# Four of the 24 modulation blocks weighed on VectorE instead of TensorE, in a two-block transformer kernel on one core

## What is computed

```python
ada = jax.nn.silu(c) @ w_ada[l] + b_ada[l]          # c: (1, 2048), w_ada: (2048, 12288)
sh1, sc1, gt1, sh2, sc2, gt2 = jnp.split(ada, 6, axis=-1)
h = modulate(rmsnorm(x, norm1_g[l]), sh1, sc1)
proj = h @ w_in[l]                                  # pool, k, v, indexer and q columns
...                                                 # indexer top-k, attention, multi-scale pool
mix = jnp.concatenate([attn_out, pool_out], axis=-1) @ w_out[l]
x = x + gt1[:, None, :] * mix
h2 = modulate(rmsnorm(x, norm2_g[l]), sh2, sc2)
x = x + gt2[:, None, :] * hier_moe(h2, w_grp[l], w_exp[l], w1[l], w3[l], w2[l])
```

## Time and profile before

| what | value |
|---|---|
| median of 3 runs | 2362.9 us (2359.02, 2363.03, 2362.9) |
| the profiled execution, its own time | 2358.78 us |
| its span | 2356.5 us |
| TensorE busy over the span | 2081.6 us (88%) |
| VectorE busy over the span | 1254.1 us (53%) |
| share of the ending chain | TensorE 49%, DMA 34%, VectorE 9% |
| TensorE modulation units in stage A | 672 matmuls into psO, 96 into psM |

### The profile page before, as it was taken

The page is one execution under the profiler, slowest core; times in us unless marked ns, Lnnn a source line. Parts: engine busy times, 40 slices in busy tenths (PEclk is TensorE's granted clock), DMA queues, the critical chain, the costliest instruction groups (busy, mean ns, idle before and its releaser), DMA issues.

```text
span 2356.5 us, 38378 instructions
## 1 busy us (share of the span) xinstructions
PE 2081.6 (88%) x14534; PEld 1353.8 (57%) x14534; DVE 1254.1 (53%) x2281; ACT 857.6 (36%) x1308; POOL 32.4 (1%) x32
## 2 busy tenths in 40 slices
PE   6899999989988888888888888999998999997997
PEld 2677767762222222222222223998887999997887
DVE  3546567554444444444444445558856554477655
ACT  3343344431111111111111114457854444466543
POOL 0000000000000000000000001011100000000000
PEclk9999999999999999999999999999998999999999
DMA  9998987889999999999999998553444455543442
GB/s 360 381 345 297 310 274 247 305 324 394 427 428 428 427 427 428 427 427 427 428 427 427 428 428 341 195 184 125 140 151 155 142 180 183 176 141 103 140 135 92
DMA packets 135046, 695.42 MB, mean 295 GB/s; under 512 B 14992, under 2 KB 15120, under 8 KB 85264
## 3 DMA queue, kind: packets, MB, share of 16 engines
q1 hardware_dynamic: 134928, 693.79, 76.5%
HBM read 691.63 MB, written 2.10 MB: 294 GB/s over the span
## 4 chain that ended last, share of the span: by engine, by line
PE 49%; DMA 34%; DVE 9%; ACT 4%; SPq 3%; issue 2%; DVEq 0%; ACTq 0%
PE acc L1174 33%; DMA ring<-in_w 30%; DMA land<-in_stream_a 3%; PE psO L1226 3%; PE psS L1457 3%; PE acc L1171 3%; DVE WL L1924 2%; SPq L1035 2%; ACT WH L1616 1%; DMA land<-in_stream_bc 1%; PE psM L1443 1%; PE acc L1443 1%; ACT SB L1701 1%; PE psT L1110 1%; PE psO L1118 0%
## 5 line engine op out<-in xcount | busy, mean ns | idle before, releaser
L1174 PE MATMUL acc<-HH,WH 128*128 128x256 f32 x2408 | 705.3, 293 | 24.6 <-DVE HL L1950 9.9
L1174 PE MATMUL acc<-HH,WL 128*128 128x256 f32 x2408 | 687.0, 285 | 0.0
L1174 PE MATMUL acc<-HL,WH 128*128 128x256 f32 x2408 | 686.7, 285 | 0.0
L1924 DVE TENSOR_TENSOR WL<-land,WH 128x1024 fp32r<-128x1024 f32 (+2 forms) x346 | 416.3, 1205 | 415.2 <-ACT WH L1616 411.3
L1174 PEld LDWEIGHTS acc<-HH,WH 128*128 128x128 f32 x2408 | 468.1, 194 | 49.9 <-issue 11.6
L1174 PEld LDWEIGHTS acc<-HH,WL 128*128 128x128 f32 x2408 | 468.3, 194 | 1.9 <-issue 1.0
L1174 PEld LDWEIGHTS acc<-HL,WH 128*128 128x128 f32 x2408 | 467.6, 194 | 0.0
L1616 ACT ACTIVATE WH<-land 128x1024 fp32r<-128x1024 f32 (+2 forms) x350 | 362.3, 1037 | 225.3 <-PE acc L1174 180.1
L1457 PE MATMUL psS<-ring,low 128*32 128x512 f32 x2048 | 274.3, 608 | 105.1 <-DMA ring<-in_w 100.5
L1457 PEld LDWEIGHTS psS<-ring,low 128*32 128x32 f32 x2048 | 40.8, 108 | 316.2 <-DMA ring<-in_w 284.8
L2331 DVE TENSOR_TENSOR X<-acc,X 128x512 f32<-128x512 f32 x128 | 88.5, 691 | 219.0 <-PE acc L1443 219.0
(11 more groups left out here) (361 smaller groups left out, 2112.9 us busy)
## 6 DMA issues: line engine op xcount, KB each, us to landing
ring<-in_w SPq DMA_DIRECT2D x384, 1024.0 KB, 26.0
land<-in_stream_a SPq DMA_DIRECT2D x284, 512.0 KB, 7.3
land<-in_stream_bc SPq DMA_DIRECT2D x246, 512.0 KB, 4.0
land<-in_stream_bc SPq DMA_DIRECT2D x12, 384.0 KB, 3.4
X<-in_xT SPq DMA_DIRECT2D x1, 2048.0 KB, 13.0
out<-low SPq DMA_DIRECT2D x4, 512.0 KB, 2.6
cst<-in_const SPq DMA_DIRECT2D x1, 1514.5 KB, 11.5
low<-in_w_pool SPq DMA_DIRECT2D x1, 1024.0 KB, 8.2
```

What stands on the lines that cost most here:

```text
L1174: mm = pe.matmul(bank[:, 0:S], w[:, kk, :], h[:, rows[kk], :], start=(z == 0 and i == 0), stop=stop)
L1924: ins = dve.tensor_tensor(wl, src, wh, ALU.subtract)
```

## The change

Blocks 8, 10, 12 and 14 are computed by VectorE. For each chunk of 128 rows of the weights, VectorE multiplies the 128x512 tile by the column of `silu(c)` that belongs to it and adds it to a 128x512 accumulator in PTS, so a unit is four dependent instructions. When all 16 chunks are done, the sum over the 128 partitions is left; TensorE makes it with four matmuls whose stationary operand is a 128x128 part of the accumulator and whose moving operand is one column of ones. VectorE then only adds the bias.

The order of the units becomes (8,0), (9,0), (8,1), (9,1), ...: one VectorE unit, one TensorE unit. The transfers of a VectorE unit are put into the list at its call; the instructions that use them are put into VectorE's list at the next call (`weigh_landed`). A finished VectorE block waits in `weighed` until the TensorE block beside it is finished, and both are turned, one right after the other, in front of the second unit of the next TensorE block (`turn_all`): 9 and 8 before (11,1), 11 and 10 before (13,1), 13 and 12 before (15,1), 15 and 14 before (16,1).

```diff
+ADA_DVE = (8, 10, 12, 14)
+ADA_PE = (*ADA_FIRST, *(b for b in range(8, 24) if b not in ADA_DVE))
...
+    def turn():
+        b = whole.pop(0)
         o.add("pe", "adaT", b)
         o.add("dve", "adaT", b)
...
+    def weigh_landed(left_over):
+        while len(landing) > left_over:
+            b, q = landing.pop(0)
+            o.add("dve", "ada", b, q)
+            if q == 3:
+                weighed.append(b)
...
     def ada(b, q):
+        by = "dve" if b in ADA_DVE else "pe"
+        if q == 1 and by == "pe":
+            turn_all()
...
         for h in range(2):
-            o.piece(("ada", b, q), h, HALF, "pe", "ada", b, q)
+            o.piece(("ada", b, q), h, HALF, by, "ada", b, q)
+        if by == "dve":
+            landing.append((b, q))
+            return
         o.add("pe", "ada", b, q)
         if q == 3:
             o.add("act", "evac", ("ada", b))
+            whole.append(b)
+            whole.extend(weighed)
+            weighed.clear()
...
-    left = [(b, q) for b in (*ADA_FIRST[4:], *range(8, 24)) for q in range(4)]
+    left = [(b, q) for b in ADA_FIRST[4:] for q in range(4)]
+    left += [(b + z, q) for b in ADA_DVE for q in range(4) for z in range(2)]
+    left += [(b, q) for b in range(16, 24) for q in range(4)]
...
     def between(rate=ADA_RATE[1]):
         owed[0] += rate
+        weigh_landed(0)
...
...
-                        if step[1] != ADA_FIRST[0]:
-                            needs(k, "dve", o, "adaT", ada_before(step[1]))
+                        if b in ADA_DVE:
+                            needs(k, "dve", o, "ada", b, 3)
+                        else:
+                            needs(k, "act", o, "evac", ("ada", b))
+                        if n:
+                            needs(k, "dve", o, "adaT", turns[n - 1])
...
+                            if b in ADA_DVE:
+                                mm = pe.matmul(bank[:, c:c + 1], weighed_rows(b)[:, P * c:P * c + P], ones[:, 0:1],
+                                               start=True, stop=True, skip_group_check=True)
...
+                        for i, p in enumerate(o.pieces_of["ada", b, q]):
+                            dve.wait_ge(unit_in[k][p % LAND[k]], 16 * (p // LAND[k] + 1))
+                            w = land[k][:, p % LAND[k], :].rearrange("p (c n) -> p c n", c=2)
+                            for z in range(2):
+                                c = 4 * q + 2 * i + z
+                                if c == 0:
+                                    ins = dve.tensor_scalar(g, w[:, z, :], cs[:, c:c + 1], None, ALU.mult)
+                                else:
+                                    ins = dve.scalar_tensor_tensor(out=g, in0=w[:, z, :], scalar=cs[:, c:c + 1], in1=g,
+                                                                   op0=ALU.mult, op1=ALU.add)
```

More of the change, by code:

```diff
@@ L385, in order_a, with turn_all @@
     shared = [False]
-    def ada_t(b):
+    whole = []
+    landing = []
+    weighed = []
+    def turn():
+        b = whole.pop(0)
         o.add("pe", "adaT", b)
         o.add("dve", "adaT", b)
+    def turn_all():
+        while whole:
+            turn()
+    def weigh_landed(left_over):
[4 more added lines that the diff above has]
+                weighed.append(b)
     def ada(b, q):
-        if q == 1 and b != ADA_FIRST[0] and ("adaT", ada_before(b)) not in o.at["pe"]:
-            ada_t(ada_before(b))
+        by = "dve" if b in ADA_DVE else "pe"
+        if q == 1 and by == "pe":
+            turn_all()
         if q == 0 and shared[0]:
@@ L461, in between @@
         owed[0] += rate
-        b = ada_before(left[0][0]) if left and left[0][1] == 0 else None
-        if shared[0] and b is not None and ("adaT", b) not in o.at["pe"]:
-            ada_t(b)
+        weigh_landed(0)
+        if shared[0] and whole and left and left[0][1] == 0:
+            turn()
             return
@@ L477, in shifts @@
         elif ("adaT", 3) not in o.at["pe"]:
-            ada_t(3)
+            turn()
             modulate(3)
@@ L527, in order_a @@
     index()
-    assert not idx
-    ada_t(23 - len(left) // 4)
+    assert not idx and left[0][0] >= 16
+    weigh_landed(0)
+    whole.extend(weighed)
+    weighed.clear()
+    turn_all()
     shared[0], owed[0] = True, 0.0
@@ L552, in order_a @@
             o.split_mix("wo", 1)
-            if ("adaT", 23 - len(left) // 4) not in o.at["pe"]:
-                ada_t(23 - len(left) // 4)
+            turn_all()
             o.add("dve", "cols")
@@ L566, in order_a @@
             o.add("dve", "shiftW")
-        if not left and ("adaT", 23) not in o.at["pe"]:
-            ada_t(23)
+        if not left and whole:
+            turn_all()
             o.add("dve", "gt2rows")
@@ L1184, in run @@
                 idx = [s[1] for s in o.steps["pe"] if s[0] == "idx"]
+                turns = [s[1] for s in o.steps["pe"] if s[0] == "adaT"]
                 def bank_of(step):
@@ L1961, in run @@
                         a = ada[:, 4 * b:4 * b + 4]
+                        if b in ADA_DVE:
+                            ins = dve.tensor_tensor(a, bankT[1][:, 0:4], C("b_ada", 4 * b, 4), ALU.add)
+                            ins.then_inc(done[k]["dve"], 1)
+                            count += 1
+                            continue
                         then(dve.tensor_reduce(a, (psM[:, :] if b in o.small_bank else bankT[1]).rearrange("p (c r m) -> p c r m", c=4, m=CAP)[:, :, :, 0],
@@ L1964, in run @@
                         ins = dve.tensor_tensor(a, a, C("b_ada", 4 * b, 4), ALU.add)
+                    elif what == "ada":
+                        _, b, q = step
+                        n = ADA_DVE.index(b)
+                        g = weighed_rows(b)
+                        if q == 0 and n > 1:
+                            needs("pe", "adaT", ADA_DVE[n - 2])
+                        for i, p in enumerate(o.pieces_of["ada", b, q]):
[5 more added lines that the diff above has]
+                                    ins = dve.tensor_scalar(g, w[:, z, :], cs[:, c:c + 1], None, ALU.mult)
+                                else:
+                                    ins = dve.scalar_tensor_tensor(out=g, in0=w[:, z, :], scalar=cs[:, c:c + 1], in1=g,
+                                                                   op0=ALU.mult, op1=ALU.add)
+                                if (i, z) != (1, 1):
+                                    then(ins)
                     elif what == "h1":
```

17 lines of the change are left out of this document (10 added, 7 removed).

## The result

The changed kernel takes 2416.15 us (median of 4 runs, 2408.37 to 2416.90); the kernel before, timed beside it, 2362.97 us (4 runs, 2359.02 to 2364.11). The ratio is 1.0223, interval 1.0208 to 1.0238: 53 us slower. The direction was forecast, the size was not: 2383 was predicted, with 2366 to 2394 as range. The profiled execution took 2416.9 us, with a span of 2414.6.

What follows compares the result with a forecast made beforehand. TensorE was taken to bound the kernel up to 331 us, VectorE from 347 us; 39.1 us added less 17.0 removed made 22 us slower, 2381 from the profiled 2358.8, plus 2 for the median: 2383 us, range 2366 to 2394.

Steps and rivals of the forecast that it cites:

- Removed: On TensorE: sixteen units at 1.1 us, one giving nothing, and a transfer wait of 0.5 us; 17.0 us saved.
- VectorE's unit: On VectorE: four dependent instructions at 0.75 us plus 0.03 link, 3.14 us a unit, 49 us in all, beside TensorE's work.
- The double turns: Before (11,1), (13,1), (15,1), (16,1): second turn waits for VectorE's adaT; 6.2, 6.2, 5.8, 4.5 us, together 22.7.
- Sums over partitions: On TensorE: eight 128x1 matmuls take 0.85 us against 0.53 for four transposes; four times 0.3, 1.3 us.
- kw rotary: TensorE's wait for VectorE's rotary step of kw: 2.7 us more, growing from 2.8 to 6.7 us.
- The clock: Lower TensorE clock behind three double turns and the kw wait: 1.6 us each, 6.4 us (bounds 0 and 8).
- The landing slots: VectorE units free two slots later; TensorE waits 2 to 3 us at four units; 6 us taken (0 to 10).
- rival 2: VectorE becomes the bound of the stretch (10%): some 0.5 us for each of ten projections; 2388 to 2396 us.
- rival 3: Even (7%): transfers are the true bound from 160 to 331 us; within 4.7 us of before.
- Rival 1: Waits real but smaller (22%): clock does not fall, slots come in time, VectorE's units cheaper; 2363 to 2370 us.
- Rival 4: Faster (6%): a second turn costs only small steps and the signal, 0.5 us; 14 us faster, 2348.
- rival 5: Data not landed at the next call, VectorE waits with everything behind it; no own size, counted with rival 2.

Runs made afterwards that it cites:

- e1: The changed kernel with 9 extra matmuls (last pair: 13) on TensorE between the two turns of each pair, results overwritten; 2405.20 us, ratio 1.0196.
- e5: The changed kernel with each VectorE unit in VectorE's list at its own call, not one call later; 2390.13 us, ratio 1.0115.
- e9: The change with three VectorE blocks (12 units), units weighed at their own call, spread among TensorE's, each turn in its own call; 2360.99 us, ratio 0.9991.
- e11: e9 with one multiply-add per VectorE unit in place of four, products of three of four chunks left out; 2354.93 us, ratio 0.9976.
- e4: The changed kernel with both turns put into the lists ahead of the VectorE unit of the same call; 2399.70 us, ratio 1.0176.
- e8_hold: The kernel before, with landing slots of 16 of 32 units of blocks 8 to 15 given back only at the next call's WL; 2363.67 us, ratio 1.0000.
- e10_four: As e9 but with all four VectorE blocks (16 units), two VectorE units for each TensorE unit; 2365.12 us, ratio 1.0017.
- e7_pairs: The kernel before, all units on TensorE, every second block's turn from 8 to 14 put off, back to back with the next; 2382.15 us, ratio 1.0076.

## Why the prediction was wrong in size

- **What bounds the kernel**: right. TensorE's list was the path up to wp0: the waits put on it, with the clock behind them, add up to the added time within 2 us.
- **Removed**: 1.1 us for a unit is borne out as far as the ledgers close with it; it was not measured by itself.
- **VectorE's unit**: 3.12 us measured, 3.14 forecast; 752 ns for one operation, 0.75 taken. (Sixteen units at 3.14 are 50 us, not 49; the sum doesn't use it.)
- **The double turns**: right in place and size: 6.16, 6.16, 5.74 and 8.53 us against 6.2, 6.2, 5.8 and 8 to 9. The working (WL, unit, two small steps, signal) is to be seen row by row in VectorE's timeline. The 4.5 us for the last one is a slip in the adding: 341.94 + 0.9 + 4.2 + 0.5 is 347.5, so 4.9 us and 23.1 in all; the measured 22.2 lies as near.
- **Sums over partitions**: 1.7 against 1.3, as the price of eight small matmuls (0.85 us) was worked out from a row of four and their next step; they took 0.95.
- **kw rotary**: 6.0 us against 6.7.
- **The clock**: the term that failed most, 24.8 us instead of 6.4 (bounds 0 to 8). Two things were wrong in it. First the number of places: the "four new waits" were ten places, nine of them new and the tenth behind q7. The clock was charged to three turns and kw alone, not to the fourth turn (behind q7), to the slot waits of the next term, or to the index step. The prediction took the wait of 2.8 us that had no loss behind it as a limit, which was one sample; waits of 2.51, 2.58, 3.01, 3.22 and 3.30 us had it. Then the price: it was 2.5 us on average (25.3 / 10), and 2.6 where it could be measured clean (e1), not 1.6. My 1.6 came from one stretch; four of the ten cost that (1.64 to 1.70 us), the other six 2.8 to 3.8, and what decides between the two was not found. The Trainium skill (TensorE: Matmul & The Clock Gate, "Why this matters for your kernels") says that idle gaps between bursts of matmuls bring the lower clock back; the prediction applied this to too few gaps, and the trace agrees with its direction at all ten.
- **The landing slots**: 17.1 us instead of the 5.5 in the sum (6 - 0.5, bounds of the 6 being 0 to 10). The mechanism, a slot freed a call and a unit later, was right (e5). The size fell short twice. The prediction's own working, 2 to 3 us at four units, makes 8 to 12 us, and it took 6 without a reason. And it left out that the queue issues in order: one held slot delays every piece behind it, TensorE's own units among them, up to 10.77 us against the 6.46 in the earlier trace rows, and the first such wait came at 171 us, ahead of where I looked.
- **Not foreseen**: 3.2 us before the index step, which waits for a rotary step that in VectorE's list now stands behind a unit, and 1.0 us of a wait for ScalarE.
- **The rivals**: VectorE as the bound (rival 2) did not happen; it did no more per microsecond than before (30.22 of 50). The transfers as the true bound (rival 3) fell for this order, since their share went from 0.94 to 0.65; for the repaired ones (e9 and e11, share 0.95) they may be part of the bound, which no run isolates. Rival 1 took the opposite side of the true error. Rival 4 (a second turn costs 0.5 us) fell with the four waits of 5.7 to 8.5 us, and rival 5 with VectorE's units, which ran where they were meant to.

Of the miss of 32 us (53.7 against 22), 18 are clock, 12 slots and 4 the small waits; the other terms together, -1, and the ledger's own gap, -2, take a little off. The range was too narrow because the bounds of clock and slots were each set from one row, and the two go together: each new wait brings its clock with it.

## What to carry to other kernels

Count every wait that a reordering makes on the busiest engine, and charge each its length plus the slow stretch behind it; here that was 2.5 us on average, and 1.6 to 3.8 us at single places, for waits of 2.5 to 8.5 us, in no order with their length. So many short waits can cost more than a few long ones of the same sum, and halving a wait's length (e4) gave back only the length. Before putting work on an engine with idle time on average, find what stands behind it in that engine's list and who waits for that: two steps that share a bank need a call of their own between them, and a buffer that an in-order queue refills has to come free when it did before. The same work in a better order took back all of the 53 us, and showed that in this stretch moving it gained nothing.

## What the runs showed of the hardware

- The granted clock can drop from 1.00 to 0.50 behind a wait of 2.27 us (e1, 231 us), and stay at 1.00 behind another of 2.27 us (e1, 280 us). The kw rotary wait of 2.8 us had no loss in the kernel before, in e8_hold and in e10_four; the same wait, 2.87 us, in e7_pairs has 0.63 in the window from 186 to 190 us, and those of e9 and e11 (2.81 us) have it too. The shortest single wait with a drop behind it was 1.85 us (e1, 330 us). Length alone does not decide in this range; what does was not found.
- TensorE's busy time times (1 - clock) was 1.6 to 3.8 us behind each of the ten waits of the changed kernel, and 1.6 to 1.9 in all five of e7_pairs, one of which stands behind a wait of 8.54 us.
- Eight 128x1 fp32 matmuls took 0.95 us up to the next step, where four 128x128 transposes took 0.53; at the lower clock 1.77 (282.09 to 283.86).
- A scalar_tensor_tensor of 128x512 fp32 took 752 ns, on the line through its 128 and 256 column forms to 1 ns.
